# Dilated projection tiles computed in pairs with seven half-depth units instead of eight

## The reference, cut to what matters

```python
DIL_PATTERN = ((128, 1), (512, 4), (2048, 16))      # three groups: window, dilation
DIL_HEADS_PER_GROUP = 8; DIL_HEAD_DIM = 128
def dilated_mixer(h, w_in, w_out):
    proj = h @ w_in                                  # 1024 x 1024 by 1024 x 10240
    q, k, v = ...                                    # each (S, 3 groups, 8 heads, 128)
    z = proj[..., 3 * DIL_QKV:]                      # the gate, 1024 wide
    for g, (window, dilation) in enumerate(DIL_PATTERN):
        o, l = dilated_window_attention(q[:, :, g], k[:, :, g], v[:, :, g], slopes[g], window, dilation)
    wts = softmax over the three groups of their log-denominators
    o = sum(wts * outs)
    return (o * silu(z)) @ w_out
```

## Time and profile before

| | |
|---|---|
| executions, us | 2904.6, 2905.06, 2903.54 (median 2904.6) |
| span of the profiled execution, us | 2902.8, which is 1.8 under the median of the runs |
| PE busy / weight loads busy | 2792.1 (96%) / 2166.9 (75%) |
| DVE, ACT, POOL busy | 1184.7 (41%), 902.8 (31%), 1022.5 (35%) |
| dilated passes | 8 exponentials per head; heads begin every 137.4 us |
| granted TensorE clock | 0.98 over the span, 1.00 in the dilated passes |

### The profile page before, as it was taken

The page is one execution under the profiler, slowest core; times in us unless marked ns, Lnnn a source line. Parts: engine busy times, 40 slices in busy tenths (PEclk is TensorE's granted clock), DMA queues, the critical chain, the costliest instruction groups (busy, mean ns, idle before and its releaser), DMA issues.

```text
span 2902.8 us, 41142 instructions
## 1 busy us (share of the span) xinstructions
PE 2792.1 (96%) x16908; PEld 2166.9 (75%) x16908; DVE 1184.7 (41%) x2813; ACT 902.8 (31%) x1701; POOL 1022.5 (35%) x447
## 2 busy tenths in 40 slices
PE   7999998899999999998999999999999999999998
PEld 5766675567777777776887878888888888887887
DVE  6989997556433333335335011111112121114323
ACT  5322413552333343344123122222222222224112
POOL 2542481133322222223632433333333333333531
PEclk8999998999999999999999999999999999999999
DMA  4110121121211111112121111111111111113211
GB/s 114 39 30 22 30 69 51 48 91 38 67 51 38 38 50 52 52 44 95 58 79 53 56 39 37 50 39 44 37 51 45 37 44 44 44 42 141 66 51 65
DMA packets 221334, 155.56 MB, mean 54 GB/s; under 512 B 25254, under 2 KB 207948, under 8 KB 221020
## 3 DMA queue, kind: packets, MB, share of 16 engines
q1 hardware_dynamic: 210076, 122.55, 14.6%
q10 hardware_dynamic: 11072, 30.39, 3.0%
HBM read 133.45 MB, written 19.47 MB: 53 GB/s over the span
## 4 chain that ended last, share of the span: by engine, by line
PE 51%; DVE 2%; issue 1%; ACT 1%; DMA 0%; ACTq 0%; DVEq 0%
PE proj L904 14%; PE proj L906 14%; PE proj L905 14%; PE out L1423 2%; PE score L1371 1%; PE score L1401 1%; PE score L1380 1%; PE proj L944 1%; PE out L905 0%; PE out L906 0%; PE out L904 0%; PE out L1390 0%; DMA y_scratch<-arena 0%; DVE arena L2343 0%; DVE arena L2470 0%
## 5 line engine op out<-in xcount | busy, mean ns | idle before, releaser
L904 PE MATMUL proj<-act_hi,w_hi 128*128 128x512 f32 x2560 | 1033.7, 404 | 10.4 <-ACT hT L1846 4.4
L906 PE MATMUL proj<-act_hi,w_lo 128*128 128x512 f32 x2560 | 1005.8, 393 | 0.0
L905 PE MATMUL proj<-act_lo,w_hi 128*128 128x512 f32 x2560 | 1005.3, 393 | 0.0
L777 POOL TENSOR_TENSOR w_hi<-w_raw,ones 128x1024 fp32r<-128x1024 f32 x175 | 420.6, 2403 | 1598.6 <-PE proj L906 1596.4
L904 PEld LDWEIGHTS proj<-act_hi,w_hi 128*128 128x128 f32 x2560 | 486.3, 190 | 122.8 <-issue 17.2
L906 PEld LDWEIGHTS proj<-act_hi,w_lo 128*128 128x128 f32 x2560 | 485.3, 190 | 104.7
L905 PEld LDWEIGHTS proj<-act_lo,w_hi 128*128 128x128 f32 x2560 | 486.6, 190 | 95.8 <-issue 0.2
L779 POOL TENSOR_TENSOR w_lo<-w_raw,w_hi 128x1024 fp32r<-128x1024 f32 x175 | 432.2, 2470 | 13.7
L1846 ACT ACTIVATE arena<-proj 128x512 f32<-128x512 f32 x236 | 175.9, 754 | 669.5 <-PE proj L906 645.5
L2470 DVE SCALAR_TENSOR_TENSOR arena<-arena,score 128x256 f32<-128x256 f32 (+1 forms) x192 | 76.1, 427 | 717.7 <-PE score L1371 676.9
L1872 ACT ACTIVATE arena<-score 128x512 f32<-128x512 f32 (+3 forms) x264 | 115.7, 486 | 197.9 <-PE score L1232 197.4
(11 more groups left out here) (268 smaller groups left out, 2874.1 us busy)
## 6 DMA issues: line engine op xcount, KB each, us to landing
w_raw<-dil_w_in_dram SPq DMA_DIRECT2D x80, 512.0 KB, 3.7
w_raw<-fox_w_in_dram SPq DMA_DIRECT2D x32, 512.0 KB, 4.1
w_raw<-w_in_dram SPq DMA_DIRECT2D x23, 512.0 KB, 3.8
y_scratch<-arena ACTq DMA_DIRECT2D x21, 512.0 KB, 3.6
act_lo<-y_scratch SPq DMA_DIRECT2D x21, 512.0 KB, 6.2
arena<-decay_scratch ACTq DMA_DIRECT2D x16, 512.0 KB, 5.9
w_raw<-ple_w_gate_dram SPq DMA_DIRECT2D x16, 512.0 KB, 3.7
arena<-x_dram SPq DMA_DIRECT2D x12, 512.0 KB, 5.0
```

The source lines that it names most:

```text
L777: pool.tensor_tensor(hi, raw, one.unsqueeze(1).broadcast_to([P, KB, P]), ALU.mult).then_inc(w_hi_done, 1)
L904: pe.matmul(bank, hi, a_hi, start=first, stop=False)
L905: pe.matmul(bank, hi, a_lo, start=False, stop=False)
L906: return pe.matmul(bank, lo, a_hi, start=False, stop=last)
```

## The change

Head 0 is projected as before. For heads 1 to 7 the ten tiles are taken as five pairs, 35 pairs in all. Weights of a pair are four quarters (first or second 512 rows, first or second tile), activations four quarters (first or second 512 channels, first or second 512 tokens). Seven products of quarters and of sums of quarters (Strassen's scheme in Winograd's form) give the four outputs. A unit is one such product: 4 row blocks x 3 = 12 matmuls, on bank `proj[j % 2]`; units 2, 4 and 6 accumulate on what is already in their bank. What else is done:

- DVE and ACT form three sums of activations and their parts once, during head 0's projection (`operand_sums`, `operand_hi`), and a fourth that overwrites a quarter of `act_hi` and `act_lo`.
- SP loads each pair as four transfers of 256 KB into quarters of `w_raw`. POOL makes per pair four sums, three hi parts and seven lo parts, 14 operations of 128x512; ACT makes the other four hi parts (128x512, from SBUF).
- ACT copies four outputs of a pair out of the banks; DVE adds five more contributions in place, the last from SBUF to SBUF.
- Seven units fill two steps (four in an even step, three in an odd one); the fifth pair of head p is computed in the opening of pass p. In a step, two units (in odd steps too: 4 and 5) come before the scores of groups 1 and 2, and the rest between them and the values.
- q is stored by token class, so the scores of group 0 too are issued as four matmuls with 32-column stationaries.
- The three transpositions of v are each issued whole (`turned_values`): in step 6, in the next opening, and in step 0 after it.
- The heads' q, k, v and gate live in 15 rotating buffers; the gated output is written over the gate, and stored from there.
- The read-back of y and the split of the output weights wait until all units are done.

```diff
+SUM_ROLES = ((("q", 0), ("q", 1)), (("q", 2), ("k", 0)), (("k", 1), ("vT", 0)), (("k", 2), ("vT", 1)), (("g", 0), ("vT", 2)))
+UNITS = 7
...
+def step_units(p, t):
+
+    first = UNITS * (len(SUM_ROLES) * p + t // 2)
+    return [first + j for j in (range(4) if t % 2 == 0 else range(4, UNITS))]
...
+            def quarter_parts(n, raw, count):
+
+                hi, lo = quarter(n)
+                later(pool, ST, "unit", n - 3)
+                pool.tensor_tensor(hi, raw, ones[:, :].unsqueeze(1).broadcast_to([P, KB // 2, P]), ALU.mult).then_inc(ST["ps"], 1)
+                later(pool, ST, "ps", count)
+                quarter_lo(n, raw)
...
+            def tile_pair(m):
...
+                quarter_by_act(n, x11, 4 * m + 1)
+                quarter_by_act(n + 1, x12, 4 * m + 2)
...
+                pool.tensor_tensor(s1, x21, x22, ALU.add).then_inc(ST["ps"], 1)
+                later(pool, ST, "ps", 7 * m + 1)
+                pool.tensor_tensor(s2, s1, x11, ALU.subtract).then_inc(ST["ps"], 1)
+                pool.tensor_tensor(x21, x11, x21, ALU.subtract).then_inc(ST["ps"], 1)
+                later(pool, ST, "ps", 7 * m + 2)
+                quarter_parts(n + 2, s2, 7 * m + 4)
+                later(pool, ST, "lo", n + 3)
+                pool.tensor_tensor(s2, x12, s2, ALU.subtract).then_inc(ST["ps"], 1)
+                quarter_by_act(n + 3, x22, 4 * m + 3)
+                quarter_parts(n + 4, x21, 7 * m + 6)
+                later(pool, ST, "ps", 7 * m + 5)
+                quarter_parts(n + 5, s2, 7 * m + 7)
+                quarter_by_act(n + 6, s1, 4 * m + 4)
...
+                def unit(n):
...
+                    later(pe, ST, "lo", n + 1)
...
+                    for k in range(KB // 2):
+                        begin, end = k == 0 and j not in (2, 4, 6), k == KB // 2 - 1
+                        pe.matmul(bank, hi[:, k], a_hi[:, k], start=begin, stop=False, skip_group_check=True)
+                        pe.matmul(bank, hi[:, k], a_lo[:, k], start=False, stop=False, skip_group_check=True)
+                        mm = pe.matmul(bank, lo[:, k], a_hi[:, k], start=False, stop=end, skip_group_check=True)
+                    mm.then_inc(ST["unit"], 1)
+
+                def turned_values(x):
+
+                    p, g = x // 3 + 1, x % 3
+                    done = len(SUM_ROLES) * (p - 1) + g + 3
+                    later(pe, ST, "ea", 4 * done)
+                    later(pe, ST, "ed", 5 * done)
...
-                            if kind == "dil" and g > 0:
-                                for u in range(DIL_CLASSES):
+                            for u in range(DIL_CLASSES):
...
                     for t in range(N):
...
                         transposes(t, 1)
-                        if pieces == 2 and t + 1 < N:
+                        if t == 6 and follow:
+                            turned_values(3 * p)
+                        if t + 1 < N:
                             scores(t + 1, 1)
-                        if follow:
-                            project(p + 1, part1)
+                        if t == 0 and p > 0:
+                            turned_values(3 * (p - 1) + 2)
+                        for n in units[:2]:
+                            unit(n)
...
-                        if follow:
-                            project(p + 1, part2)
                         if t + 2 < N:
                             scores(t + 2, 0)
...
+                        for n in units[2:]:
+                            unit(n)
...
+                        values(t, 0)
+                        values(t, 1)
...
+                    places = {0: (0, 0, 1.0), 2: (0, 1, 1.0), 3: (1, 0, -1.0), 6: (1, 1, 1.0)}
...
+                    places = {1: ((0, 0, 1.0),), 4: ((1, 0, 1.0), (0, 1, -1.0)), 5: ((0, 1, 1.0),)}
...
+                    if j == 6:
...
+                        later(dve, ST, "ea", 4 * m_ + 4)
...
+                        dve.scalar_tensor_tensor(dst, other, scale / own, dst, ALU.mult, ALU.add).then_inc(ST["ed"], 1)
...
-    nc = bacc.Bacc("TRN2", target_bir_lowering=False, num_devices=1)
+    nc = bacc.Bacc("TRN2", target_bir_lowering=False, num_devices=1, dynamic_dma_scratch_size=1024)
```

More of the change, by code:

```diff
@@ L174, in plain, with heads @@
             c += 1
-    def heads(kind):
+    def heads(kind, count=None):
         nonlocal c
-        for _ in range(PASSES[kind]):
+        for _ in range(PASSES[kind] if count is None else count):
             for what in ORDER[kind]:
@@ L493, in build @@
         DL.line()
+        slots = [DL.take(T) for _ in range(DIL_SLOTS)]
         sparse_rows = [G4.take(T) for _ in range(4)]
@@ L684, in finished_rows @@
                 m = MIXER[kind]
-                for half in range(2):
-                    sp.wait_ge(pass_done[half], base + PASSES[kind] * len(ORDER[kind]) - (1 if kind == "dil" else 0))
+                if kind == "dil":
+                    later(sp, ST, "unit", UNITS_ALL)
+                else:
+                    for half in range(2):
+                        sp.wait_ge(pass_done[half], base + PASSES[kind] * len(ORDER[kind]))
                 sp.wait_ge(AT[kind]["ysent"], 16 * (STORES_BEFORE[kind] + PASSES[kind] - 2))
@@ L1169, in out_rows @@
                     pe.wait_ge(w_split, n + 1)
-                    for half in range(2):
-                        wait(pe, pass_free[half], c)
+                    later(pe, ST, "ea", 4 * TILE_PAIRS)
+                    later(pe, ST, "ed", 5 * TILE_PAIRS)
+                    later(pe, ST, "xe", 2 * turned_before(TILE_PAIRS))
                 for j in js:
@@ new lines, in one @@
+                    if p == 0:
+                        for half in range(2):
+                            act.wait_ge(pass_free[half], base + NB)
+                        exp(0)
+                        act.wait_ge(pass_done[1], base + 12)
+                        for k in range(KB // 2):
+                            later(act, ST, "tv", 10 * (k + 1))
+                            act.activation(act_hi[:, k, 512:1024], fourth[k], ACT.Copy).then_inc(ST["th"], 1)
+                        gate()
+                    else:
+                        opening = opening_units(p)
+                        values_turned(3 * (p - 1) + 1)
+                        unit_out(opening[0])
+                        exp(0)
+                        for n in opening[1:4]:
+                            unit_out(n)
+                        wait_pass(act, S["y"], p, NT, 0)
+                        at = (p - 1) * P + rows
+                        act.dma_start(yd[at:at + P, :], sets["dil"][p - 1]["g"]).then_inc(S["ysent"], 16)
+                        for n in opening[4:]:
+                            unit_out(n)
@@ L1959, in attention @@
                         projected(0, 0, [(0, half, None), (1, half, None)])
-                halves = [(b, half, None) for b, half in (PAIR_HALVES if kind != "dil" else product(range(NB), range(2)))]
+                    for b in range(2, NB):
+                        projected(0, 0, [(b, half, None) for half in range(2)])
+                        if 3 <= b < 3 + KB // 2:
+                            operand_hi(b - 3)
+                    for n in range(4):
+                        quarter_hi(n)
+                halves = [(b, half, None) for b, half in PAIR_HALVES]
                 if kind == "dsa":
```

488 lines of the change are left out of this document (338 added, 150 removed).

## The result

The changed kernel takes 2884.07 us (median of 4 executions, 2883.25 to 2884.59) beside 2904.07 us for the kernel before on the same chip (2903.43 to 2905.06): ratio 0.9929, 95% interval 0.9915 to 0.9943. It is faster by 20 us; I had forecast 48 (2856 us, with a range of 2834 to 2880). The direction was right, the size was not: the time lies 4 us above the range.

What follows compares the result with a forecast made beforehand. PE was taken as the bound, busy 137.25 of 137.40 us per head. Products -95.3, borders +29, waits +16, start and end +2 gave -48 us: 2856 us, range 2834 to 2880.

Steps and rivals of the forecast that it cites:

- the products: PE's projection: 84 matmuls per pair of tiles instead of 96, 420 fewer at 0.227 us each, -95.3 us.
- the borders: PE's changes between whole-array work and 32 columns around group 0's scores and values: +29 us, 15 to 38.
- the nearest are 0.69 for two SBUF operands with POOL still and 1.26 beside POOL: Price range in us for DVE's last addition, SBUF to SBUF, which the trace did not show.
- The rule that I weighed: DVE with both inputs in SBUF and GpSimd reading SBUF exclude each other; would end the waits' sum 9 us higher.
- Step 6 has values, turn and six transposes ahead (2.5) and a plain copy (0.60): nothing.: Transposition of v in step 6: 2.5 us of PE work cover its chain, so no wait there.
- if the clock leaves its full level: Sign that would show the forecast wrong: the clock falling from its full level; no size given.
- start and end: Openings of the kernel and its output tail after the last unit: together +2 us.
- the waits: PE's waits for transpositions of v: about 0.8 us per opening, 1.3 in step 0; 16 us in all, 10 to 25.
- Borders and waits free: Rival: changes of tile shape and waits for v cost nothing; 2820 us, chance 12%.
- Evictions pace the units: Rival: emptying banks by ACT and DVE holds up units, about 1 us a pair, +35, 2891 us; chance 17%.
- POOL sets the pace: Rival: POOL's 14 operations per pair slow to 2.28 us each and bound the heads, +193, 3098 us; chance 6%.
- No effect: Rival: starting units behind PE's waits costs 0.2 us each, 245 of them take back the 48 us; 2905 us, chance 3%.

Runs made afterwards that it cites:

- e2: Changed kernel with the scores of group 0 as one matmul of 128 columns lying together (other rows than the reference's): 2880.32 us, ratio 0.9916.
- e3: Changed kernel with all of a step's units behind the scores of the step after next: 2889.74 us, ratio 0.9954.
- e6: Changed kernel with the edits of e1 and e2 together: 2849.86 us, ratio 0.9815.
- e5: Changed kernel with DVE's last addition of each pair on operands that lie together, its result then wrong: 2879.15 us, ratio 0.9910.
- e1: Changed kernel where PE transposes v without waiting for DVE's last addition; in openings the new head's scores wait for it: 2863.17 us, ratio 0.9856.
- e7: Changed kernel with e1, e3, e4, step 0's v transpositions behind step 2's scores, DVE's last addition behind the next step's sums and maximum: 2848.34 us, ratio 0.9808.
- e4: Changed kernel with step 6's transpositions of v behind the scores of step 7: 2881.75 us, ratio 0.9919.
- e9: e7 with two units again ahead of the scores of step 2 in head 0's step 0: 2842.69 us, ratio 0.9778.

## Why the prediction was wrong

**Right: the products.** 420 went, and they still stand 0.227 apart inside a unit: -95.3 us, 13.6 per head.

**Right: the borders.** Forecast 29 us. With 5.2 us of waits (next points: 1.4 + 1.9 + 0.4 + 0.6 + 0.9, each from where the instruction would have started to where it did) a head's borders come to 133.6 - 137.4 + 13.6 - 5.2 = 4.6 us, 32 in all. That is a remainder; what was measured by itself is the price of a block: 0.33 in e2's rows and 0.31 in e3's busy times where I had 0.29, and e6 shows that this is real time.

**Wrong: "the nearest are 0.69 for two SBUF operands with POOL still and 1.26 beside POOL, ends I keep (a strided write could add to either)."** This is the step that failed. The remark in brackets stood beside the range and not in it, although showed the strided factor for ACT (1.05 for 0.60), and I used it for a rival only. Two prices add up. The stride costs 0.3 to 0.4 us (e5). Company of POOL costs up to 1.06 (2.14 against 1.08). I had read the second from one group's mean, 1.26. With an addition of 1.45 the opening's wait was 1.41 for 0.8, and with 1.42 step 0's was 1.9 for 1.3; the later wait for ACT's copy was 0.42, as forecast.

The rule that I weighed (the Trainium skill, SBUF — State Buffer, Who interferes with whom) would have come nearer. By it DVE's addition would begin when POOL's L981 ends at 2014.45 (2013.17 + 1.28) and end 1.08 later, at 2015.53; it ended at 2015.39. POOL's L1013 would then end 1.29 after DVE, at 2016.68; it ended at 2016.55. The trace agrees to 0.15 us. In the opening and in step 0 the addition met a POOL operation (L992) that had 0.6 us left; the same working ends it at 2070.06 and 1961.47, and it ended at 2069.86 and 1961.22. So the company cost 0.34 to 0.37 us at the 13 places for which the forecast, counting a whole operation, put 0.7 and thus 9 us more in all. Nearly a whole one it met ahead of step 6, where I had counted no wait.

**Wrong, and part of the same term: "Step 6 has values, turn and six transposes ahead (2.5) and a plain copy (0.60): nothing."** There are 0.6 and 0.9 us. The first is again the addition, 2.11 us long at this pair, with 0.44 + 0.60 ahead of it. The second is a wait that I did not list: ACT's copy of v into a rotating buffer waits for the scores that still read it, and PE issues those behind the transposition. The change had that wait in its code (`values_turned`); 15 buffers make each new tile the successor of a certain old reader, and I never asked which.

**Wrong, small: "if the clock leaves its full level".** I had it as a sign and gave it no price. It fell in one full head, +1.6 us, and also at the start of head 0 (0.83 over 20 us) and in the last head (0.94 from 2611 to 2640 us, behind 2.51 us of wait in its step 0).

The sum by what was measured, from the profiled spans: products -95.3, borders 32, waits 5.2 x 7 = 36, clock 1.6 give -25. The span fell by 21.3, so start and end hold the other 4, where I had 2. From the eighth exponential of the last head to the end both kernels take the same, 218.1 and 218.2 us, so nothing was lost behind it. Head 0's start had 1.4 us more of wait, and a mean clock of 0.83 over 20 us is the lower level for 6.8 of them, at most 3.4 us of work lost (an estimate from the rows of 1690 to 1710); the last head's low stretch comes on top. That can hold the 4, but no run tested it.

Of the 27 us between forecast and profile 20 are the waits, 36 for 16. By the places above some 12 are the chain with DVE's addition (opening, step 0, step 6), 6 are ACT's blocked copy, and 2 the last head's step 0, which I had not counted. e1 gave back as much, 21 us, with one number; but it took the addition out of the chain altogether, the part that I had forecast included, so that the two numbers agree is luck.

**The rivals.** Borders and waits free: no, both cost. Evictions pace the units: no; where nothing parts the four units of a step (step 6, from 2045.50 to the values at 2056.55) they take 11.05 us, 10.9 of them for 48 products, so no gap is left for a bank. POOL sets the pace: no wait of PE is for it, though it makes DVE's addition long. No effect: no.

## What to carry over

Ask of each wait what the waiting instruction really reads: the counter was one too high, since the last event counted only another tile. An operation that the profile does not show is priced with its strides and with the neighbour that it will meet, both added, and when it stands in a chain that nothing covers, the range must hold the sum. If a step is made shorter ahead of a fixed chain, the wait grows and the gain is not seen until the chain goes: test such edits together (e6, e7), not only alone (e2, e3).

## What the hardware showed that I had not expected

- PE's wait in step 0 can lower the clock behind it, and the same wait may or may not. Counted over six heads each, the granted clock fell in one behind 1.82 us idle (the changed kernel), in three behind 1.80 to 1.82 (e4), in one behind 1.80 (e3), in one behind 1.54 (e5) and in six behind 1.94 (e2); with waits of at most 0.81 us in a full head (e1, e6 to e9) it never did. Once down it cost 3 to 8 products at 0.42 to 0.43 us, 1.0 to 1.6 us. What decides is not shown.
- An addition by DVE of 128x512 from PSUM, in place, scattered over the four token classes (neighbours 256 columns apart) takes 1.10 us, and 0.69 where the columns lie together; 1.0 in the mean of the 140. ACT's copy goes from 0.60 to 1.08 with the same pattern.
- One scalar_tensor_tensor on SBUF operands takes 1.08 us with POOL idle and 2.14 beside it, and POOL pays too (2.02 for 1.29).
